# The Hyena gate's slabs ahead of x0's, the forward transform by even and odd times, and the heads' squares on ScalarE

## The reference

```python
z_hy, q, k, v, gates = split(h @ w_in)            # x0, x1, v of z_hy by a short convolution
u = v * x1
uf = rfft(u, n=2 * L); kf = rfft(k, n=2 * L)      # k: the Hyena kernel, made of a small network
y_hy = ((irfft(uf * kf)[:L] + u * hy_bias) * x0) @ w_hy_out
o = softmax(q1 k1) v - lam * softmax(q2 k2) v     # 8 heads, keys also from a context of 256
y_da = (rmsnorm_2(o, subln_g) * (1 - lam_init)) @ w_da_out
g_hy, g_da = split(sigmoid(gates))
out = (g_hy * y_hy + g_da * y_da) @ w_o
```

## Time and profile before

| | |
|---|---|
| time, 3 runs | 1277.33 us median (1277.33 to 1279.48) |
| the profiled execution | 1278.81 us, its span 1277.0 us |
| mean granted TensorE clock | 0.997 |
| TensorE busy | 1244.6 us, 97% |
| VectorE busy | 853.7 us, 67% |
| ScalarE busy | 581.0 us, 45% |
| GpSimd busy | 101.9 us, 8% |
| DMA | 219.27 MB, mean 172 GB/s |

### The profile page before, as it was taken

How to read it: one execution, slowest core, us unless ns; L and a number is a source line. 1 busy time by engine, 2 the same in 40 slices (tenths; PEclk the granted TensorE clock), 3 DMA queues, 4 the chain that set the end, 5 groups by cost and what they waited for, 6 DMA issues and landing times.

```text
span 1277.0 us, 19283 instructions
## 1 busy us (share of the span) xinstructions
PE 1244.6 (97%) x7697; PEld 1097.6 (86%) x7697; DVE 853.7 (67%) x1328; ACT 581.0 (45%) x926; POOL 101.9 (8%) x101
## 2 busy tenths in 40 slices
PE   6999999999999999999999999999999999999997
PEld 6897999988888888887787998888788997999986
DVE  5886888797787777753424876357877676555544
ACT  6746545445622223222324752246345645444533
POOL 2040001100000000001100013001430000000000
PEclk9999999999999999999999999999999999999999
DMA  8444577776375568862342442333233553655562
GB/s 326 139 149 154 195 246 241 239 246 204 127 229 191 193 240 292 290 213 100 99 148 74 149 157 93 98 116 116 86 97 109 188 173 126 199 182 182 183 196 83
DMA packets 59752, 219.27 MB, mean 172 GB/s; under 512 B 6844, under 2 KB 7136, under 8 KB 58896
## 3 DMA queue, kind: packets, MB, share of 16 engines
q1 hardware_dynamic: 56736, 205.42, 49.2%
q0 software_dynamic: 2352, 11.76, 2.6%
q10 hardware_dynamic: 576, 0.88, 0.2%
HBM read 216.95 MB, written 1.07 MB: 171 GB/s over the span
## 4 chain that ended last, share of the span: by engine, by line
PE 86%; DVE 6%; ACT 5%; issue 2%; DMA 1%; POOL 0%; DVEq 0%; ACTq 0%
PE ps L2104 19%; PE ps L2106 18%; PE ps L2105 18%; PE ps L2152 4%; PE ps L2154 4%; PE ps L2153 4%; PE ps L2163 3%; PE ps L2165 3%; PE ps L2164 3%; ACT hi L697 2%; PE ps L2141 1%; PE ps L2140 1%; PE ps L2142 1%; PE ps L2632 1%; PE ps L2654 1%
## 5 line engine op out<-in xcount | busy, mean ns | idle before, releaser
L1301 DVE TENSOR_TENSOR lo<-raw,hi 128x1024 fp32r<-128x1024 f32 x315 | 389.8, 1238 | 291.2 <-ACT hi L697 290.9
L2104 PE MATMUL ps<-nh,hi 128*128 128x256 f32 (+1 forms) x1776 | 552.6, 311 | 8.3 <-DVE u L1412 2.9
L2106 PE MATMUL ps<-nl,hi 128*128 128x256 f32 (+1 forms) x1776 | 545.4, 307 | 0.0
L2105 PE MATMUL ps<-nh,lo 128*128 128x256 f32 (+1 forms) x1776 | 545.3, 307 | 0.0
L697 ACT ACTIVATE hi<-raw 128x1024 fp32r<-128x1024 f32 x315 | 332.7, 1057 | 448.2 <-PE ps L2106 248.4
L2104 PEld LDWEIGHTS ps<-nh,hi 128*128 128x128 f32 x1776 | 340.2, 192 | 38.8 <-issue 19.1
L2105 PEld LDWEIGHTS ps<-nh,lo 128*128 128x128 f32 x1776 | 340.4, 192 | 16.2 <-issue 1.0
L2106 PEld LDWEIGHTS ps<-nl,hi 128*128 128x128 f32 x1776 | 340.3, 192 | 15.4
L711 ACT ACTIVATE sg<-ps 128x256 f32<-128x256 f32 (+1 forms) x66 | 30.1, 456 | 132.1 <-PE ps L2106 132.0
L1288 DVE SCALAR_TENSOR_TENSOR raw<-raw,cvec 128x1024 f32<-128x1024 f32 x72 | 86.8, 1222 | 1.4
L1313 DVE TENSOR_TENSOR sg<-sg,ps 128x256 f32<-128x256 f32 (+1 forms) x66 | 33.6, 509 | 59.8 <-PE ps L2106 59.8
(11 more groups left out here) (373 smaller groups left out, 1318.4 us busy)
## 6 DMA issues: line engine op xcount, KB each, us to landing
raw<-in_up SPq DMA_DIRECT2D x132, 512.0 KB, 4.0
raw<-in_in SPq DMA_DIRECT2D x86, 512.0 KB, 3.5
raw<-in_w_ada SPq DMA_DIRECT2D x72, 512.0 KB, 4.6
raw<-in_down SPq DMA_DIRECT2D x66, 512.0 KB, 3.7
raw<-in_out SPq DMA_DIRECT2D x8, 512.0 KB, 3.7
raw<-in_hy_out SPq DMA_DIRECT2D x8, 512.0 KB, 3.8
raw<-in_da_out SPq DMA_DIRECT2D x8, 512.0 KB, 4.2
raw<-in_o SPq DMA_DIRECT2D x8, 512.0 KB, 3.5
```

The costliest lines, as they stand in the source:

```text
L1301: dve.tensor_tensor(lo[:, h, 0:w], raw[:, r, 0:w], hi[:, h, 0:w].bitcast(F32), ALU.subtract).then_inc(lo_done, 1)
L2104: mm(o, hi[:, h, wk], x_hi, start=first, stop=False)
L2105: mm(o, lo[:, h, wk], x_hi, start=False, stop=False)
L2106: return mm(o, hi[:, h, wk], x_lo, start=False, stop=last)
```

## The change

The order becomes `hy_v`, `gate_hy`, `hy_x0`, `gate_da`, `hy_out`. The two gates get tiles of their own: the Hyena gate's lies over `kT`, so a copy waits for the scores that read that part. u is transposed by even and by odd times. A forward transform turn is now a kind (cosine or sine) of one half of the channels: two products, of the even and the odd times, each into a bank of its own. ScalarE copies the odd one to `uodd`; VectorE makes sum and difference, which are the lower and upper frequencies, and multiplies each by the two parts of the kernel's spectrum. GpSimd adds up after the second kind. The transforms stand at p = 10, 12, 14, 16, `inverse`, `convolved` and the rounding of the result one slab later. The squares of the heads are summed by ScalarE behind `take_out` instead of VectorE. The constant `dft` has 8 tiles instead of 16.

```diff
-SPECTRUM_AT = (10, 12, 14, 15)
+SPECTRUM_AT = (10, 12, 14, 16)
...
-WOVEN = ("hy_v", "hy_x0", "gate_hy", "gate_da", "hy_out")
+WOVEN = ("hy_v", "gate_hy", "hy_x0", "gate_da", "hy_out")
...
+            for half in range(2):
                 w = slice(half * 512, half * 512 + 512)
...
+                for ft in range(2):
+                    kr, ki = (k[:, ft, w].rearrange("p (a n) -> p a n", a=2) for k in (kre, kim))
+                    re, im = halves(proj, ft, half), halves(spec_im, ft, half)
+                    pool.wait_ge(sem("u_products"), 8 * half + 2 * ft + 6)
+                    pool.tensor_tensor(re, re, ki, ALU.subtract).then_inc(sem("yf_ready"), 1)
+                    pool.tensor_tensor(im, im, kr, ALU.add).then_inc(sem("yf_ready"), 1)
...
+                act.wait_ge(sem("otok_ready"), r + 1)
+                if r:
+                    act.wait_ge(sem("oss_ready"), r)
+                act.activation(rtmp[:, 0:P], otok[:, r, :], ACT.Square,
+                               accum_out=small[:, 192 + r:193 + r]).then_inc(sem("oss_ready"), 1)
...
+                        if name == "gate_hy":
+                            act.wait_ge(sem("s2_ready"), 2 * (x.j // 2) + 2)
+                        elif x.j == 0:
+                            act.wait_ge(sem("yf_ready"), 8)
...
+                    if p in SPECTRUM_AT:
+                        g = SPECTRUM_AT.index(p)
+                        act.wait_ge(sem("uf_ready"), g + 1)
+                        if g >= 2:
+                            act.wait_ge(sem("u_folded"), g - 1)
+                        act.activation(uodd[:, g % 2, :], ps[:, 3, :], ACT.Copy).then_inc(sem("uodd_copied"), 1)
...
-                    if p == 27:
+                    if p == 28:
                         act.wait_ge(sem("yhy_ready"), KD)
...
+                dve.wait_ge(sem("uodd_copied"), g + 1)
+                if g == 0:
                     dve.wait_ge(sem("kernel_folded"), 4)
...
+                step(dve.tensor_tensor(flat(low), ps[:, 2, :], uodd[:, g % 2, :], ALU.add))
+                dve.tensor_tensor(flat(high), ps[:, 2, :], uodd[:, g % 2, :], ALU.subtract)\
+                   .then_inc(sem("u_folded"), 1)
                 after(n)
...
+                dve.wait_ge(sem("u_folded"), g + 1)
+                for ft, part in enumerate((low, high)):
+                    kr, ki = (k[:, ft, w].rearrange("p (a n) -> p a n", a=2) for k in (kre, kim))
+
+                    to = (halves(spec_im, ft, half), halves(proj, ft, half)) if kind == 0 else (ki, kr)
+                    for k, y in zip((ki, kr), to):
+                        dve.tensor_tensor(y, k, part, ALU.mult).then_inc(sem("u_products"), 1)
...
+                y = st["hy_x0"][j]
+                dve.wait_ge(bank_free[y.bank], y.use + 1)
...
-                    if 3 <= p <= 33 and p % 2:
-                        square_sum((p - 3) // 2)
-                    if p == 28:
+                    if p == 29:
...
-                                     u[:, 4 * half + j, tt * P:tt * P + P], ident)
+                                     u[:, 4 * half + j, tt:T:2], ident)
...
+                half, kind = g // 2, g % 2
                 pe.wait_ge(sem("ut_copied"), 4)
                 if g:
...
+                    pe.wait_ge(sem("u_folded"), g)
+                for odd in range(2):
+                    o = mm(ps[:, 2 + odd, :], dft[:, 2 * kind + odd, :], ut_half(odd, half), start=True, stop=True)
                 o.then_inc(sem("uf_ready"), 1)
...
-                    if 17 <= p < 25:
-                        inverse(p - 17)
+                    if 18 <= p < 26:
+                        inverse(p - 18)
```

More of the change, by code:

```diff
@@ L384, in build @@
         x0 = place(8 * KB, "x0", [P, KD, T])
-        gT = place(16 * KB, "gT", [P, 2 * KD, T])
+        g_hy = place(58 * KB, "g_hy", [P, KD, T])
+        g_da = place(24 * KB, "g_da", [P, KD, T])
         rope = place(32 * KB, "rope_s", [P, 2, T])
@@ L651, in _ @@
                     .then_inc(sem("u_ready"), 1)
-            for g in range(4):
-                half, ft = g // 2, g % 2
+            for half in range(2):
                 w = slice(half * 512, half * 512 + 512)
[L655 to L669, removed]
+                for ft in range(2):
[4 more added lines that the diff above has]
+                    pool.tensor_tensor(im, im, kr, ALU.add).then_inc(sem("yf_ready"), 1)
+                pool.wait_ge(sem("yf_ready"), 4 * half + 4)
+                for m, y in enumerate((proj, spec_im)):
+                    low, high = halves(y, 0, half), halves(y, 1, half)
+                    pool.tensor_tensor(ut_half(m, half), low, high, ALU.add).then_inc(sem("folded"), 1)
+                    pool.wait_ge(sem("folded"), 4 * half + 2 * m + 1)
+                    pool.tensor_tensor(high, low, high, ALU.subtract).then_inc(sem("folded"), 1)
             pool.wait_ge(sem("o2_ready"), 2 * HEADS2)
@@ L1919, in spectrum, with flat @@
             def spectrum(g):
-                half, ft = g // 2, g % 2
-                pair = "p (a n) -> p a n"
+                half, kind = g // 2, g % 2
                 w = slice(half * 512, half * 512 + 512)
[L1923 to L1929, removed]
+                low, high = (yt[:, 2 * n:2 * n + 2, :] for n in range(2))
+                def flat(a):
+                    return a.rearrange("p a n -> p (a n)")
+                dve.wait_ge(sem("uodd_copied"), g + 1)
+                if g == 0:
                     dve.wait_ge(sem("kernel_folded"), 4)
-                step(dve.tensor_tensor(t0, kr, ur, ALU.mult))
-                dve.tensor_tensor(t1, ki, ui, ALU.mult).then_inc(sem("re_products"), 1)
+                step(dve.tensor_tensor(flat(low), ps[:, 2, :], uodd[:, g % 2, :], ALU.add))
+                dve.tensor_tensor(flat(high), ps[:, 2, :], uodd[:, g % 2, :], ALU.subtract)\
+                   .then_inc(sem("u_folded"), 1)
                 after(n)
-                dve.wait_ge(sem("re_products"), g + 1)
-                step(dve.tensor_tensor(ki, ki, ur, ALU.mult))
-                dve.tensor_tensor(kr, kr, ui, ALU.mult).then_inc(sem("im_products"), 1)
+                dve.wait_ge(sem("u_folded"), g + 1)
[4 more added lines that the diff above has]
+                        dve.tensor_tensor(y, k, part, ALU.mult).then_inc(sem("u_products"), 1)
             def convolved(j):
@@ L1974, in _ @@
                         spectrum(SPECTRUM_AT.index(p - 1))
[L1975 to L1978, removed]
+                    if 19 <= p < 27:
+                        convolved(p - 19)
                     if late:
```

44 lines of the change are left out of this document (15 added, 29 removed).

## The result

The changed kernel takes 1280.59 us (median of 18 runs, 1278.78 to 1282.19), the kernel before, run beside it, 1278.70 us (18 runs, 1277.27 to 1280.22): a ratio of 1.0015 [1.0009, 1.0021]. It is 1.9 us slower, within the 0.2% that I called no difference, and the forecast was +1.5 us. The profiled execution took 1280.47 us with a span of 1278.7, where that of before took 1278.81 with 1277.0.

A forecast was written before the change was run, and what follows sets the result against it. TensorE was taken as the bound, 86% of the span, with VectorE close behind. Savings of 9.6 us against 11.1 us of new waits gave +1.5 us, a median of 1278.8 us; range 1273.5 to 1282.0.

The forecast's parts named there:

- Removed: TensorE's woven stretch: halved forward transform products save 6.9 us and two vanished waits for VectorE 2.7, together 9.6 us.
- the two old waits: TensorE's waits for VectorE at the fourth transform, 1.53 us, and slab 17, 1.17; forecast to go, saving 2.7 us.
- TensorE's loop: TensorE's time per two slabs with one forward transform turn: forecast 10.04 us, against 10.5 for VectorE, which falls behind 0.5.
- hit: A VectorE operation with two SBUF inputs lengthened by meeting GpSimd's folds; forecast at 1.1 us each.
- Costed at nothing: Strided loads for transposing u (at most about 2 us) and gate copies waiting for scores; both taken as 0 us.
- Squares and tables: ScalarE's 16 added squares at 0.4 us each, with no table load between Square and Exp; rival table loads: net +9, 0.01.
- The port: VectorE's SBUF operations and GpSimd's folds shut each other out in the woven stretch; 1.1 us taken per collision.
- The walk: VectorE's and ScalarE's queues followed through the woven stretch: new TensorE waits 2.5 + 0.5 + 4.9 + 1.9 + 1.3 = 11.1 us.
- Net: Whole kernel: 9.6 us saved against 11.1 us of new waits, +1.5 us; median forecast 1278.8 us, chance 0.50.
- The clock rival: TensorE's clock slows after slab 19's 4.9 us wait, losing 1.7; net +3.2, 1280.5 us; slower cases together 0.28.
- Unhindered products: Rival: the 16 spectrum products on VectorE are not slowed by GpSimd; -3 us, 1274.2 us, chance 0.13.
- a VectorE never late: Rival: no collision costs VectorE and its queue has slack; -7.2 us, 1270.1 us, chance 0.09.

The follow-up runs named there:

- one-column folds: The changed kernel with GpSimd's 16 spectrum operations on one column of each half, leaving out most of the convolution's result: 1270.60 us, ratio 0.9933 to the kernel before.
- the PSUM form with the old order: The changed kernel with u's sum and difference written to PSUM, x0's rounding at p = 27 and 28, old slab order: 1273.70 us, 0.9963 against before.

## Why the prediction was right, point by point

- **Removed, 9.6 us.** 6.9 forecast, 6.84 found; the two old waits went in that form, 2.7. TensorE's loop was put at 10.04 us and is 10.05. VectorE's was put at 10.5 and is 10.28 (sums at 894.18 and 904.46, ahead of any hit), so it loses 0.2 a loop and not 0.5; its first block started 0.3 later than the walk has it, and by the second block the two errors cancel.
- **Costed at nothing.** Right, with a footnote: the strided stationary operand does load slower, 0.209 us where it was 0.140 (median of 16), and no wait of TensorE followed. The gate copies made no wait. The squares have a place that I did not look at: the last of them delays what ScalarE does ahead of the heads' normalisation, 0.5 us.
- **Squares and tables.** The step is 0.40 us (0.31 and a read of 0.19, starting at 992.00 and followed at 992.31 by x0's rounding), no table load stands between square and exponential in the stretch, as the earlier trace rows promised. The prediction says that the trace disagrees there with the Trainium skill (ScalarE: Activation LUTs, "Table sets: the hidden batching unit"); but the lists of functions given there end in dots and rule nothing out, so the trace only adds Square to them.
- **The port.** The price of a hit, 1.1, is 1.08 and 1.09 for products and 1.06 to 1.09 for remainders, and both sides wait in turn. Seven hits were forecast; six of them came, and four others. Two causes: I took operations with two SBUF tensors as the only ones exposed, and L1918 (+1.04 and +1.03) is none; and I left out the mixing (+0.49 and +0.46). Against it the third block was not hit: GpSimd was done at 920.70, and its first product starts at 920.83. That is a miss by 0.1 us on the lucky side.
- **The walk.** By row, forecast and found: maps of p=15 0 and 0.90; maps of p=17 2.5 and 1.00; slab 18 0.5 and 0.42; slab 19 4.9 and 5.45; slab 21 1.9 and none, with 1.29 of slow clock in its place; maps of p=31 1.3 and 0.88. The first two are the error of the hits: L1918 and the mixing made the maps of p=15 late, the unhit third block gave it back, and those of p=17 were mixed at 928.58 where the walk has 928.6; TensorE, held up at p=15, wanted them later than forecast. Their sum, 11.1, is 9.94 found, and with the heads' 0.5 it is 10.4.
- **Net.** +1.5 forecast, +1.7 between the spans, +1.9 between the medians. The time itself was put at 1278.8 us and is 1280.6, since the kernel before took 1278.7 beside it and not the 1277.3 of its first three runs. (The forecast's own range, 1276 to 1280.5, is a slip: the 2.6 us either way that stand beside it are 1274.7 to 1279.9 around 1277.3; the range as a whole does not rest on it.) Part of that closeness is errors that cancel: 1.2 too much of waits, 0.5 too little at the heads, 0.5 in the gaps around waits, and 0.2 at the start that no run ties to the change. The walk's places are partly luck as well: at the first fold the hits that I missed, 1.5 us, and the one at the third block that did not come, 1.1, nearly cancel.
- **The clock rival** happened as its text has it, as a mechanism: the clock fell after the wait ahead of slab 19, and the wait of slab 21 took the loss up, 1.3 us where I had put 1.7. Slab 21's bank is free at 952.56 (the taps of 952.08) and slab 21 starts at 952.71, so it cost next to nothing on top. The run with the squares on VectorE shows the other side of that sentence: there 2.3 us were lost, more than the wait behind could take up, and slab 21 started 0.9 us after its bank was free. The Trainium skill (TensorE: Matmul & The Clock Gate, "Why this matters for your kernels") warns of idle gaps; here the waits of 5.70, 5.45, 3.43, 3.39, 3.38 and 2.30 us in this stretch were each followed by the 1.2 GHz level, those of 1.53, 1.42 and 1.28 were not.
- **The rivals that fell.** Unhindered products (1274.2) and a VectorE never late (1270.1): both describe kernels that the experiments made, not this one. With one operand in PSUM the products are unhindered and the time is 1276.5; with the folds all but gone it is 1270.6.

## What to carry to other kernels

Work taken off the bounding engine pays only as far as the next engine can follow, so walk the follower's queue with the lengths that its operations have beside their neighbours, not their lengths alone. Where GpSimd works in SBUF, look through every VectorE operation of that time, small scalings too, for those that took longer beside it here: two tensors in SBUF, or a scaling from SBUF to SBUF. Leave one operand in PSUM where it already stands there. A long wait can take the clock with it, and what that costs depends on the next wait: 1.3 us of slow clock ahead of a wait of about the same length cost next to nothing, 2.3 us cost 0.9.

## What the runs showed of the hardware

- A `tensor_scalar` of 128x2 from SBUF to SBUF takes 0.17 us, and 1.19 to 1.26 when it starts beside a GpSimd `tensor_tensor`; one of 128x256 (`u` by a column, L1948) takes 0.35 with one-column folds and 1.36 beside a fold in the PSUM form with the old order. One of 128x1 beside GpSimd at 915.77 kept its 0.27, as the reciprocal of 128x2 at 915.57 its 0.17.
- VectorE's multiply and sum of a head (128x128, one tile read twice) goes from 0.28 to 1.35 us.
- GpSimd's 128x512 operation takes 1.27 us alone and 1.67 to 2.24 beside VectorE's. Operations that GpSimd makes on two columns take 0.19 us alone; beside VectorE's products they took 0.58 and 0.64 and beside a remainder 1.11, while the products kept their 0.68 and the remainder its 1.22: a short operation on GpSimd's side cost VectorE nothing that shows.
- A load of 128x128 FP32 weights for a transpose with a stride of two elements takes 0.209 us, without it 0.140.
